# An RWKV-7 chunk inverse by doubling: products of 32 columns in place of 64 at each level

## The reference, cut to what matters

```python
def step(S, inp):
    r_t, d_t, k_t, v_t, kk_t, b_t = inp
    sk = jnp.einsum('bhvk,bhk->bhv', S, kk_t)
    S = S * d_t[:, :, None, :] - sk[..., None] * b_t[:, :, None, :] + v_t[..., None] * k_t[:, :, None, :]
    return S, jnp.einsum('bhvk,bhk->bhv', S, r_t)
```

## Time and profile before

| | us |
|---|---|
| median of 3 runs | 4223.6 (4220.27 to 4229.66) |
| the profiled execution | 4226.71, of which the span 4225.1 |
| TensorE busy in the span | 4024.9 (95%) |
| VectorE busy | 3163.1 (75%) |
| ScalarE busy | 1440.3 (34%) |
| GpSimd busy | 1302.4 (31%) |
| RWKV prompt phase in the span | about 718 to 1026 |
| granted TensorE clock, mean | 0.977 |

### The profile page before, as it was taken

The page is one execution under the profiler, slowest core; times in us unless marked ns, Lnnn a source line. Parts: engine busy times, 40 slices in busy tenths (PEclk is TensorE's granted clock), DMA queues, the critical chain, the costliest instruction groups (busy, mean ns, idle before and its releaser), DMA issues. The chain is left out here.

```text
span 4225.1 us, 82817 instructions
## 1 busy us (share of the span) xinstructions
PE 4024.9 (95%) x30898; PEld 3670.8 (87%) x30898; DVE 3163.1 (75%) x6289; ACT 1440.3 (34%) x2563; POOL 1302.4 (31%) x1014
## 2 busy tenths in 40 slices
PE   8999999998679999999999998999999999999998
PEld 5998887886549979888888878999999999999997
DVE  5721434555762368887789888999999999999998
ACT  4212222223652232233378872222222222222223
POOL 5333331000122100344433324334444433444441
PEclk9999999998879999999999998999999999999999
DMA  6765575574733311344446669999999999999995
GB/s 222 227 202 188 200 235 198 226 262 128 214 114 108 124 56 36 95 143 145 139 148 207 222 207 343 301 299 301 300 299 304 301 301 300 297 304 300 302 301 191
DMA packets 532580, 928.46 MB, mean 220 GB/s; under 512 B 286848, under 2 KB 355200, under 8 KB 524816
## 3 DMA queue, kind: packets, MB, share of 16 engines
q1 hardware_dynamic: 396512, 549.91, 40.7%
q0 software_dynamic: 81056, 346.96, 24.5%
q10 hardware_dynamic: 54816, 28.85, 2.4%
HBM read 786.05 MB, written 206.30 MB: 235 GB/s over the span
## 5 line engine op out<-in xcount | busy, mean ns | idle before, releaser
L3690 POOL DMA_INDIRECT ex_rows<-expert_rows,ex_here x512 | 586.5, 1145 | 956.0 <-DVE acc_tok L3930 866.5
L3930 DVE SCALAR_TENSOR_TENSOR acc_tok<-ex_rows,ex_wsp,acc_tok 128x1024 f32<-128x1024 f32 x512 | 633.7, 1278 | 0.0
L2945 PE MATMUL ex_psa<-x_dense_high,eg_u_high 128*128 128x288 f32 x2048 | 604.5, 295 | 6.6 <-DVEq L4044 6.2
L2945 PE MATMUL ex_psa<-x_dense_low,eg_u_high 128*128 128x288 f32 x2048 | 604.5, 295 | 0.0
L2945 PE MATMUL ex_psa<-x_dense_high,eg_u_low 128*128 128x288 f32 x2048 | 604.2, 295 | 0.0
L3044 POOL TENSOR_TENSOR eg_u_low<-eg_u,eg_u_high 128x1024 fp32r<-128x1024 f32 x130 | 314.3, 2418 | 743.3 <-ACT eg_u_high L3038 743.3
L3809 ACT ACTIVATE ex_w<-ex_psa 128x288 f32<-128x288 f32 x256 | 105.4, 412 | 1058.3 <-PE ex_psa L2945 1058.3
L3722 PE MATMUL ex_pso<-ex_w_high,ex_v_high 128*128 128x288 f32 x2048 | 442.5, 298 | 18.8 <-DVE acc L3912 17.1
L3722 PE MATMUL ex_pso<-ex_w_high,ex_v_low 128*128 128x288 f32 x2048 | 440.4, 297 | 0.0
L3722 PE MATMUL ex_pso<-ex_w_low,ex_v_high 128*128 128x288 f32 x2048 | 439.1, 296 | 0.0
L3912 DVE TENSOR_TENSOR acc<-ex_pso,acc 128x576 f32<-128x576 f32 x512 | 373.8, 750 | 44.9 <-PE ex_pso L3722 44.9
(11 more groups left out here) (577 smaller groups left out, 8795.7 us busy)
## 6 DMA issues: line engine op xcount, KB each, us to landing
eg_u<-in_u SPq DMA_DIRECT2D x256, 512.0 KB, 5.5
expert_rows<-in_v SPq DMA_DIRECT2D x128, 512.0 KB, 7.0
ex_v<-in_v SPq DMA_DIRECT2D x128, 512.0 KB, 6.2
weights<-wt_stage SPq DMA_DIRECT2D x36, 1024.0 KB, 4.9
ex_g<-weights SPq DMA_DIRECT2D x128, 288.0 KB, 6.7
expert_rows<-eg_act SPq DMA_DIRECT2D x256, 128.0 KB, 1.7
proj<-in_out POOLq DMA_DIRECT2D x50, 548.5 KB, 6.2
in_w<-in_w_in SPq DMA_DIRECT2D x50, 512.0 KB, 5.1
```

Source lines behind the costliest of these rows:

```text
L2945: yield nc.tensor.matmul(out[:, 0:b - a], w[:, kc, :], half[:, kc, a:b], start=n == 0, stop=n == len(passes) - 1)
L3690: pool.indirect_dma_start(rows[i][:, :], None, table, index(here[par][:, t, j:j + 1]), element_offset=ROW_RUNS[t][0]).then_inc(s_row[i], 16)
L3930: v.scalar_tensor_tensor(out=acc_tok[:, t, :], in0=rows[i][:, at:at + D], scalar=wsp[:, i:i + 1], in1=acc_tok[:, t, :], op0=ALU.mult, op1= ...
```

## The change

All three products of a level work on 32 columns per head. Of x at level `lv` only the left halves of the blocks of 2z columns enter (`left_of_blocks`, a strided view of 32 columns in runs of z), so P and Q have 32 columns per head, packed: 128 columns for four pairs, in PSUM and in `mx`. ScalarE copies 128 columns. VectorE subtracts Q from the same strided columns of x, 128 of them. At the last level the weights are mx (64 x 32), the moving side is the right half of y, and the result has 32 partitions per half; two subtractions, one for each half of the partitions, put it into the upper right quarter of y. This last form is now bound to level 5 (`LEVELS - 1`) and not to the last of `levels`, so that the samples' last level goes the way of the others: subtraction from x, then a transposition.

```diff
--- before.py
+++ after.py
@@ -1131,10 +1131,20 @@
         self.h = h
         self.mt = sb("mt", [P, NPAIR, 256])
         self.xy = sb("xy", [P, NPAIR, 2, CL])
-        self.mx = other.mx if other else sb("mx", [P, NPAIR, CL])
+        self.mx = other.mx if other else sb("mx", [P, NPAIR, CL // 2])
         self.tmp = other.tmp if other else sb("tmp", [P, NPAIR, CL])
         self.ml = other.ml if other else sb("ml", [P, 2, NPAIR, CL])
         self.tok = sb("tok", [P, 3, NPAIR, CL])
+
+
+def left_of_blocks(ap, lv):
+    z = 1 << lv
+    return ap.rearrange("p (b h w) -> p b h w", h=2, w=z)[:, :, 0, :]
+
+
+def left_of_blocks_of_pairs(ap, lv):
+    z = 1 << lv
+    return ap.rearrange("p a (b h w) -> p a b h w", h=2, w=z)[:, :, :, 0, :]
 
 
 def rw_matrix_pe(k, b, ch, in5, levels, at):
@@ -1144,8 +1154,8 @@
     heads = [(p_, rows) for p_ in range(NPAIR) for rows in halves()]
     mt = ps[:, BANK_MT:BANK_MT + 2, :].rearrange("p a (b m) -> p (a b) m", m=256)
     tok = ps[:, BANK_TOK:BANK_TOK + 2, :].rearrange("p a b -> p (a b)")[:, 0:768].rearrange("p (q a t) -> p q a t", q=3, a=4)
-    four = lambda bank: ps[:, bank, 0:256].rearrange("p (a t) -> p a t", a=4)
-    pq = four(BANK_Q[h])
+    half = lambda bank: ps[:, bank, 0:128].rearrange("p (a t) -> p a t", a=4)
+    pm, pq = half(BANK_P[h]), half(BANK_Q[h])
     if h:
         at(DV, "mt_0")
     for p_, rows in heads:
@@ -1167,16 +1177,18 @@
             if h:
                 at(AC, "tok_1")
         for p_, rows in heads:
-            mm = nc.tensor.matmul(four(BANK_P[h])[rows, p_, :], ch.ml[rows, lv % 2, p_, :], ch.xy[rows, p_, 0, :], start=True, stop=True)
+            mm = nc.tensor.matmul(pm[rows, p_, :], ch.ml[rows, lv % 2, p_, :], left_of_blocks(ch.xy[rows, p_, 0, :], lv),
+                                  start=True, stop=True)
         mm.then_inc(*PE.inc(f"mx{lv}_{h}"))
         yield
         at(DV, f"y{lv - 1}_{h}")
         at(AC, f"mx{lv}_{h}")
         for p_, rows in heads:
-            if lv < levels - 1:
+            if lv < LEVELS - 1:
                 mm = nc.tensor.matmul(pq[rows, p_, :], ch.xy[rows, p_, 1, :], ch.mx[rows, p_, :], start=True, stop=True)
             else:
-                mm = nc.tensor.matmul(pq[rows, p_, :], ch.mx[rows, p_, :], ch.xy[rows, p_, 1, :], start=True, stop=True)
+                upper = slice(rows.start, rows.start + CL // 2)
+                mm = nc.tensor.matmul(pq[upper, p_, :], ch.mx[rows, p_, :], ch.xy[rows, p_, 1, CL // 2:CL], start=True, stop=True)
         mm.then_inc(*PE.inc(f"xmx{lv}_{h}"))
         yield
 
@@ -1189,7 +1201,7 @@
     yield
     for lv in range(1, levels):
         at(PE, f"mx{lv}_{h}")
-        nc.scalar.activation(ch.mx[:, :, :].rearrange("p a t -> p (a t)"), b.ps[:, BANK_P[h], 0:256],
+        nc.scalar.activation(ch.mx[:, :, :].rearrange("p a t -> p (a t)"), b.ps[:, BANK_P[h], 0:128],
                              ACT.Copy).then_inc(*AC.inc(f"mx{lv}_{h}"))
         yield
 
@@ -1216,17 +1228,22 @@
     at(DV, f"y0_{h}")
     v.transpose(x, y).then_inc(*DV.inc(f"x0_{h}"))
     yield
-    pq = b.ps[:, BANK_Q[h], 0:256].rearrange("p (a t) -> p a t", a=4)
+    pq = b.ps[:, BANK_Q[h], 0:128]
     for lv in range(1, levels):
         if lv < levels - 1:
             level_of_m(lv + 1)
-            at(PE, f"xmx{lv}_{h}")
-            v.tensor_tensor(x, x, pq, ALU.subtract).then_inc(*DV.inc(f"x{lv}_{h}"))
+        at(PE, f"xmx{lv}_{h}")
+        if lv < LEVELS - 1:
+            left = left_of_blocks_of_pairs(x, lv)
+            v.tensor_tensor(left, left, pq.rearrange("p (a b w) -> p a b w", a=4, w=1 << lv), ALU.subtract).then_inc(*DV.inc(f"x{lv}_{h}"))
             at(DV, f"x{lv}_{h}")
             v.transpose(y, x).then_inc(*DV.inc(f"y{lv}_{h}"))
         else:
-            at(PE, f"xmx{lv}_{h}")
-            v.tensor_tensor(y, y, pq, ALU.subtract).then_inc(*DV.inc(f"y{lv}_{h}"))
+            for rows in halves():
+                upper = slice(rows.start, rows.start + CL // 2)
+                right = y[upper, :, CL // 2:CL]
+                last = v.tensor_tensor(right, right, pq[upper, :].rearrange("p (a t) -> p a t", a=4), ALU.subtract)
+            last.then_inc(*DV.inc(f"y{lv}_{h}"))
         yield
 
 
@@ -1235,7 +1252,7 @@
     steps = [f"{s}_{h}" for h in chunks for s in ("mt", "t0", "ml1", "y0", "x0")]
     for lv in range(1, levels):
         for h in chunks:
-            steps += [f"ml{lv + 1}_{h}", f"x{lv}_{h}"] * (lv < levels - 1) + [f"y{lv}_{h}"]
+            steps += [f"ml{lv + 1}_{h}"] * (lv < levels - 1) + [f"x{lv}_{h}"] * (lv < LEVELS - 1) + [f"y{lv}_{h}"]
     return steps
 
 
```

## The result

| | before | changed |
|---|---|---|
| median, 11 runs each, us | 4220.3 | 4231.2 |
| lowest to highest, us | 4210.5 to 4229.7 | 4221.8 to 4240.0 |
| ratio (95% interval) | | 1.0029 (1.002 to 1.0038) |
| mean granted clock of the executions | 0.978 (0.975 to 0.980, in the 82 executions timed beside the experiments) | 0.972 (0.970 to 0.975) |

The forecast was 4218.0 us, 5.6 less than before; "slower by over 0.2%" had a chance of 0.07 in it.

What follows compares the result with a forecast made beforehand. TensorE's pace of issue was taken to bound the RWKV phase. Terms -1.3 - 2.4 - 0.75 - 1.5 + 0.3 = -5.6 us took the 4223.6 median to 4218.0; its own range 4214 to 4224, overall 4211 to 4227.

Steps and rivals of the forecast that it cites:

- The bound: RWKV prompt phase: goes at TensorE's pace of issue; twelve groups of issue waits, together 20 us, left as they are.
- the second rival: RWKV rounds: faster bursts only wait longer for issue, about 1.5 us gain remains, 4222 us; chance 0.10.
- Part 1: First and second products, 64 to 32 moving columns: 0.02 us gained per burst, 1.3 us in all; ends 0 and 2.5.
- the first rival: First and second products: the moving stream is the limit, bursts fall from 0.94 to about 0.5 us, 4199 us; chance 0.08.
- so halving the stream leaves the other: First and second products: stream and weight-column limits are equal at 64x64, so with fewer moving columns the weights' pace remains.
- the slower one, short strided runs: First product, levels 1 to 4: x in short strided runs streams at a quarter of the pace, 22 us, 4240; chance 0.04.
- Part 2: Last product, weights 64 to 32 columns: MATMULs at half the pace, 0.015 us each; 0.34 us per round, 2.4 in seven.
- the other case: Last product: a floor of about 25 ns per matmul would leave 0.18 us gained per round, 1.3 us.
- Part 3: ScalarE copies 277 ns, VectorE subtractions about 281: 0.75 us gained in the rounds, 1.5 in the first pair of chunks.
- The wait before u: Rounds: product u starts 0.25 us late on VectorE's rhs copy; shorter subtractions close it, 0.75 us over three rounds.
- Part 4: Added work: two last-level half subtractions cost nothing on the path; the samples' extra transposition adds 0.3 us.
- The sum: Whole kernel: all terms add up to -5.6 us, with the ends -0.8 and -7.9; forecast 4218.0 us, chance 0.76.

Runs made afterwards that it cites:

- e1: The changed kernel run again with no edit; 1.0037 of the kernel before, median 4236.7 us.
- e4: The changed kernel, but the first product moves the first 32 columns of x, contiguous, in place of the strided left halves; 1.0029 of the kernel before, 4233.9 us.
- e2: The changed kernel with first and second product moving 64 columns again, narrow copies, subtractions and last product kept; 0.9999 of the kernel before, 4217.9 us.
- e5: The changed kernel with only the first product moving 64 columns again; 0.9997 of the kernel before, 4220.8 us.
- e10b: The changed kernel with the first product back at 64 columns and four state-work products narrowed to 32; 1.003 of the kernel before, 4233.2 us.
- e3: The changed kernel with all three products moving 64 columns, the last one's weights still 32; 0.9996 of the kernel before, 4219.4 us.
- e6: The changed kernel with only the second product moving 64 columns, its 32 sent twice; 1.0003 of the kernel before, 4222.1 us.

## Why the prediction was wrong

**The bound.** Right: TensorE sets the pace of the phase. The waits on issue are what they were, twelve groups on PE from 4.2 to 0.4 us, 20.7 together against 20.4, so the second rival (gains go into issue waits) is out.

**Part 1, the step that failed.** Its first half held. The pace below 64 moving columns is set by the weights, and the burst fell from 1.15 to 1.12, between the ends that I gave, so the first rival (a burst at half) is out. The 0.03 is all pace: from the first to the last start of a burst 0.90 us in place of 0.93, while the last MATMUL still takes 0.22, where I had put half of the difference down to it. The Trainium skill's rule in "TensorE: Matmul & The Clock Gate", section LDWEIGHTS, held nearly: 53 ns for 64 columns of weights by the rule, 58 ns per tile here with 32 and with 16 moving columns (0.90 us over 31 starts, in two tiles). The failure is in "so halving the stream leaves the other", which I priced from nothing to 2.5 us gained, with no end on the other side. I read the granted clock, 0.97 in the phase, as a constant of it, and so put its price at nothing. It is a result of what TensorE does there. With 32 columns TensorE is under way as long as before but moves half as much in these products, and it spent more of the phase at the half level: a clock of 0.92 in the phase's 322.5 us (0.89 in e1), against 0.96 in 318.6 before. None of my rivals held this; the slower one, short strided runs, had the right sign and the wrong mechanism (e4).

What it costs, from the 201 timed executions of all kernels here: time against mean clock has a slope of 2.2 us per 0.001, with a correlation of -0.89. The changed kernel's mean is 0.0054 under that of the kernel before, so about 12 us by that line, and 12.2 were measured (0.29% of 4221). The line does not separate the clock's price from the gains. Among the eleven executions of the changed kernel alone the slope is 3.3, which would be 18 us of price and 6 of gain; but such slopes within one kernel go from 1.4 (e2, e5) to 4.5 (e10b), and that of the kernel before is 2.0. So the net loss is measured, 12.2 us, and the price of the clock alone is not: if the gains below came in full, it is an estimated 18.

**Part 2.** The pace was close to the half that I took: the MATMULs of a chunk start 0.017 us apart, and all 32 take 0.91 us with the wait for chunk 1's copy between. So the floor of 25 ns that I gave as the other case does not show here. From the fifth first product to rhs a clean round takes 979.77 - 977.81 = 1.96 us, against 2.21. That is 0.25 gained where I had 0.34. The missing 0.1 stands behind the last product: rhs starts 0.12 us after the start of its last MATMUL, where before it was 0.02; the trace names no releaser.

**Part 3.** 277 ns for 277 predicted, 283 for 281. The wait before u is closed: from the third first product to u 0.91 us at full clock, before 1.20. The first pair's level is 2.53 at full clock (e2), predicted 2.51, and its fifth level 0.38 shorter than before, predicted 0.37.

**Part 4.** The two half subtractions take 280 ns each as predicted, and TensorE does not wait for them. In the last round the second u waits 1.30 us for the copy of rhs, against 1.01: the +0.3 that I gave.

**The sum.** Added up where the clock is full: 63 bursts x 0.03, 1.9; seven round ends x 0.25, 1.8; three waits before u x 0.3, 0.9; first pair 4 x 0.26 and 0.38, 1.4; samples +0.3. That is -5.7 us against my -5.6. It is an estimate: only three of the seven round ends are clean, in both kernels, and the first pair's figures are e2's. So the forecast had the instructions right and left out the clock under them. That the sums agree so closely is partly luck: a smaller gain at the round ends is made up for by a larger one in the bursts. On the whole time the gain was never shown by itself: e2 and e3, which keep the copies and subtractions and most of the clock, stand at 0.9999 and 0.9996, 0 to 2 us.

No version here beats the kernel before by more than can be measured.

## What to carry to other kernels

Where the rows show that a small matmul's pace is set by its weights, its moving columns cost hardly any time of their own (here 1.15 us a burst against 1.12), but they may be what keeps the granted clock up. Before narrowing an operand, look at the clock of that stretch, and if it is already below 1.00 in places, put a bound on the slower side. If the narrowing is wanted for the engines behind (shorter copies out of PSUM), the moving side can stay wide, by sending columns twice, as in e2.

## What the runs showed of the hardware that I had not expected

- In the first pair the granted clock fell with no more waiting than before. TensorE was busy 16.9 of 18 us at a clock of 0.66, and 14.9 of 18 at 0.99 before. (In the rounds of these two kernels the falls follow waits, and the difference is in how long the clock stays down.) At 1.2 GHz its instructions take longer, so the busy share rises when the clock falls; it is no sign of activity.
- The price is not proportional. Half of the narrowing (e5, e6) cost nothing measurable, the whole 0.3%, and going on to 16 columns 0.6%. Narrowing other products of the phase (e10b) brought the 0.3% back.
- The executions of one kernel differ in clock, 0.970 to 0.975 for the changed one, and the profiled one may lie at an end: by its span alone, 4220.2 against 4225.1, the change would have looked like a gain of 5 us.
